# Gate tables built from rounded one-hots, with the gate split into a high and a low part

## What is computed

```
qry  = (x @ w_q)                                  # 8 heads, two halves of 128
s    = qry . sub_keys                             # 128 scores for each half
s_top, i_top = top_k(s, 16)                       # per half
best, pos = top_k(all 256 sums of the two, 16)    # per head
expert = i * 128 + j                              # i from the first half, j from the second
gate = softmax(best)                              # 16 per head, so 128 choices a token
hid  = gelu(x . u_tab[expert])
out  = sum over choices of gate * hid * v_tab[expert]
```

## Time and profile before

| | |
|---|---|
| median of 3 runs | 1135.03 us (1134.43 to 1135.56) |
| span of the profiled execution, first to last instruction | 1132.8 us |
| TensorE busy in the span | 1091.1 us, 96% |
| VectorE, ScalarE, GpSimd busy | 815.5, 555.7 and 589.1 us |
| stage with the gate tables | 417.8 to 750.4 us |
| mean granted TensorE clock | 0.990 of full speed |

### The profile page before, as it was taken

The page is one execution under the profiler, slowest core; times in us unless marked ns, Lnnn a source line. Parts: engine busy times, 40 slices in busy tenths (PEclk is TensorE's granted clock), DMA queues, the critical chain, the costliest instruction groups (busy, mean ns, idle before and its releaser), DMA issues.

```text
span 1132.8 us, 20715 instructions
## 1 busy us (share of the span) xinstructions
PE 1091.1 (96%) x6734; PEld 966.9 (85%) x6734; DVE 815.5 (72%) x1398; ACT 555.7 (49%) x898; POOL 589.1 (52%) x452
## 2 busy tenths in 40 slices
PE   6999999986999999999989999999999999999995
PEld 4887887675999999999989999997888888888884
DVE  4347656365899988888997888976666666666666
ACT  4347544542345555455555555554444444444442
POOL 5484345443322346666556667655555555555554
PEclk9999999997999999999999999999999999999998
DMA  6655344342545554444434444446555555555552
GB/s 200 240 187 167 130 161 137 111 149 77 166 157 182 169 180 154 162 151 165 157 124 164 149 132 146 134 161 216 192 186 185 185 186 187 187 190 193 186 186 93
DMA packets 52474, 186.51 MB, mean 165 GB/s; under 512 B 6209, under 2 KB 6593, under 8 KB 52433
## 3 DMA queue, kind: packets, MB, share of 16 engines
q1 hardware_dynamic: 51584, 182.87, 48.5%
q0 software_dynamic: 848, 3.15, 0.8%
HBM read 184.94 MB, written 1.05 MB: 164 GB/s over the span
## 4 chain that ended last, share of the span: by engine, by line
PE 84%; DVE 8%; DMA 3%; issue 2%; POOL 2%; ACT 1%; DVEq 0%; SPq 0%; POOLq 0%
PE ps L1150 15%; PE ps L1151 15%; PE ps L1152 15%; PE ps L1450 10%; PE ps L1452 10%; PE ps L1451 10%; PE ps L1410 5%; DVE wlo L717 2%; DMA raw<-w_tiles_in 1%; POOL wlo L346 1%; PE ps L1190 1%; DVE hot L1024 1%; ACT whi L482 1%; DVE sel L1029 1%; PE ps L1377 1%
## 5 line engine op out<-in xcount | busy, mean ns | idle before, releaser
L346 POOL TENSOR_TENSOR wlo<-raw,whi 128x256 fp32r<-128x256 f32 x341 | 440.2, 1292 | 497.7 <-ACT whi L482 497.2
L717 DVE TENSOR_TENSOR wlo<-raw,whi 128x768 fp32r<-128x768 f32 x341 | 361.4, 1060 | 254.5 <-ACT whi L482 253.0
L482 ACT ACTIVATE whi<-raw 128x1024 fp32r<-128x1024 f32 x344 | 364.2, 1059 | 331.4 <-DMA raw<-w_tiles_v 180.4
L1150 PE MATMUL ps<-ahi,whi 128*128 128x256 f32 x1152 | 333.5, 290 | 3.0 <-DVE wlo L717 1.6
L1151 PE MATMUL ps<-alo,whi 128*128 128x256 f32 x1152 | 326.4, 283 | 0.0
L1152 PE MATMUL ps<-ahi,wlo 128*128 128x256 f32 x1152 | 326.2, 283 | 0.0
L1150 PEld LDWEIGHTS ps<-ahi,whi 128*128 128x128 f32 x1152 | 221.4, 192 | 3.8 <-DVE wlo L717 2.0
L1151 PEld LDWEIGHTS ps<-alo,whi 128*128 128x128 f32 x1152 | 221.7, 192 | 0.0
L1152 PEld LDWEIGHTS ps<-ahi,wlo 128*128 128x128 f32 x1152 | 221.2, 192 | 0.0
L1450 PE MATMUL ps<-whi,hhi 128*128 128x512 f32 x512 | 202.4, 395 | 1.1 <-POOL wlo L346 1.1
L1451 PE MATMUL ps<-wlo,hhi 128*128 128x512 f32 x512 | 202.2, 395 | 0.0
(11 more groups left out here) (190 smaller groups left out, 998.3 us busy)
## 6 DMA issues: line engine op xcount, KB each, us to landing
raw<-w_tiles_u SPq DMA_DIRECT2D x128, 512.0 KB, 3.3
raw<-w_tiles_v SPq DMA_DIRECT2D x128, 512.0 KB, 3.3
raw<-w_tiles_in SPq DMA_DIRECT2D x64, 512.0 KB, 3.3
raw<-w_tiles_q SPq DMA_DIRECT2D x16, 512.0 KB, 3.4
raw<-w_tiles_out SPq DMA_DIRECT2D x8, 512.0 KB, 3.3
xraw<-xT SPq DMA_DIRECT2D x4, 256.0 KB, 6.3
xt<-x POOLq DMA_DIRECT2D x1, 1024.0 KB, 5.6
out<-xt SPq DMA_DIRECT2D x4, 256.0 KB, 2.0
```

Source lines behind the costliest of these rows:

```text
L346: pool.tensor_tensor(wlo[:, tile.slot, DVE_COLS:], raw[:, tile.slot, DVE_COLS:], whi[:, tile.slot, DVE_COLS:].bitcast(F32), ALU.subtract)\
L482: act.activation(whi[:, tile.slot, :], raw[:, tile.slot, :], ACT.Copy)\
L717: dve.tensor_tensor(wlo[:, tile.slot, 0:DVE_COLS], raw[:, tile.slot, 0:DVE_COLS], whi[:, tile.slot, 0:DVE_COLS].bitcast(F32), ALU.subtract)\
L1150: pe.matmul(out, ah, bh, start=start, stop=False)
```

## The change

The plain fp32 product of a token becomes two fp32r products that are summed in PSUM. The gate moves from the j side to the i side and is split: `gateT` now has the type fp32r (the rounded gate), `gate_lo` is the fp32 gate less the rounded one. The stationary `hot_j` is the bare one-hot of j, the moving operands are `hot_i`, scaled by the rounded gate, and `hot_lo`, scaled by the rest.

- GpSimd scales the i half instead of the j half (`scale_i`, the same shape).
- ScalarE copies the j half in one instruction as before, and then makes `hot_lo` with four instructions of 128 columns, one for each token, each with that token's `gate_lo` column as its per-partition scale. `hot_lo` has one buffer, so these wait until TensorE has finished the chunk before.
- VectorE computes `gate_lo` once for each half of the tokens.
- TensorE issues eight fp32r products of 128 columns for a chunk, where it issued four plain ones.
- `keys` and `iota` move in SBUF behind the PEER buffers, and `rstd`, `shift` and `gate_warm` become columns of one tensor, which makes room for `hot_lo` and `gate_lo`.

```
-        def scale_j(c):
+        def scale_i(c):
             pool.wait_ge(S["hot_ready"], c + 1)
             if c >= HOTS:
                 pool.wait_ge(S["g_done"], c + 1 - HOTS)
-            pool.tensor_tensor(hot_j[:, c % HOTS, :, :], raw_ij[:, c % HOTS, 1, :, :].rearrange("p j n -> p n j"),
-                               gateT[:, c * BLK:(c + 1) * BLK, None].to_broadcast([P, BLK, P]), ALU.mult)\
-                .then_inc(S["hot_j_ready"], 1)
+            pool.tensor_tensor(hot_i[:, c % HOTS, :, :], raw_ij[:, c % HOTS, 0, :, :].rearrange("p i n -> p n i"),
+                               gateT[:, c * BLK:(c + 1) * BLK, None].bitcast(F32).to_broadcast([P, BLK, P]),
+                               ALU.mult).then_inc(S["hot_i_ready"], 1)
...
-        def widen_i(c):
+        def hot_parts(c):
             act.wait_ge(S["hot_ready"], c + 1)
             if c >= HOTS:
                 act.wait_ge(S["g_done"], c + 1 - HOTS)
-            act.activation(hot_i[:, c % HOTS, :, :], raw_ij[:, c % HOTS, 0, :, :].rearrange("p i n -> p n i"), ACT.Copy)\
-                .then_inc(S["hot_i_ready"], 1)
+            act.activation(hot_j[:, c % HOTS, :, :], raw_ij[:, c % HOTS, 1, :, :].rearrange("p j n -> p n j"), ACT.Copy)
+            if c > 0:
+                act.wait_ge(S["g_done"], c)
+            for k in range(BLK):
+                last = act.activation(hot_lo[:, k, :], raw_ij[:, c % HOTS, 0, :, k], ACT.Copy,
+                                      scale=gate_lo[:, c * BLK + k:c * BLK + k + 1])
+            last.then_inc(S["hot_j_ready"], 1)
...
             own.do(dve.tensor_copy(gateT[:, toks], ps[:, SEL_BANKS[t], 2 * P:3 * P]))
+            own.do(dve.tensor_tensor(gate_lo[:, toks], ps[:, SEL_BANKS[t], 2 * P:3 * P], gateT[:, toks].bitcast(F32),
+                                     ALU.subtract))
...
             for k in range(BLK):
-                last = pe.matmul(ps[:, RING[b], k * P:(k + 1) * P], hot_j[:, b, k, :], hot_i[:, b, k, :],
-                                 start=True, stop=True)
+                o = ps[:, RING[b], k * P:(k + 1) * P]
+                pe.matmul(o, hot_j[:, b, k, :], hot_i[:, b, k, :], start=True, stop=False)
+                last = pe.matmul(o, hot_j[:, b, k, :], hot_lo[:, k, :], start=False, stop=True)
             last.then_inc(S["g_done"], 1)
```

More of the change, by code:

```diff
@@ L206, in layer @@
     ident = place("ident", [P, P])
-    keys = place("keys", [P, 2, NK])
-    iota = place("iota", [P, P])
     stats = place("stats", [P, NT, 2, 6])
     mv = place("mv", [P, NT, 2])
-    rstd = place("rstd", [P, NT])
-    shift = place("shift", [P, 1])
-    gate_warm = place("gate_warm", [P, 1])
+    columns = place("columns", [P, 4])
+    rstd, shift, gate_warm = columns[:, 0:NT], columns[:, NT:NT + 1], columns[:, NT + 1:NT + 2]
     work_at = at[0]
@@ L247, in layer @@
     square = place("square", [P, GDV])
-    assert at[0] <= nc.sbuf_usable_end, at[0]
+    low_end = at[0]
+    assert low_end <= nc.sbuf_usable_end, low_end
     at[0] = work_at
@@ L262, in layer @@
     hot_at = at[0]
-    hot_i = place("hot_i", [P, HOTS, BLK, P])
-    hot_j = place("hot_j", [P, HOTS, BLK, P])
+    hot_i = place("hot_i", [P, HOTS, BLK, P], F32R)
+    hot_j = place("hot_j", [P, HOTS, BLK, P], F32R)
     qs = place("qs", [P, 2, SEQ], alias=hot_at)
@@ L267, in layer @@
     selT = place("selT", [P, 2, SEQ], BF16)
-    gateT = place("gateT", [P, SEQ])
+    gateT = place("gateT", [P, SEQ], F32R)
     iota4 = place("iota4", [P, P, BLK], BF16)
@@ L275, in layer @@
     gsum = place("gsum", [P, PH])
+    late_at = at[0]
+    keys = place("keys", [P, 2, NK])
+    iota = place("iota", [P, P])
+    assert late_at >= low_end, (late_at, low_end)
+    at[0] = late_at
+    hot_lo = place("hot_lo", [P, BLK, P], F32R)
+    gate_lo = place("gate_lo", [P, SEQ])
     assert at[0] <= nc.sbuf_usable_end, at[0]
@@ L457, in _ @@
             if c is not None:
-                scale_j(c)
+                scale_i(c)
             split_lo(Tile(T_U + u + AHEAD))
@@ L681, in _ @@
             if c is not None:
-                widen_i(c)
+                hot_parts(c)
             split_hi(Tile(T_U + u + AHEAD))
```

## The result

The changed kernel takes 1139.45 us (median of 6 runs, 1137.07 to 1139.86) beside 1135.18 us for the kernel before in the same rounds: ratio 1.0036, 95% interval 1.0026 to 1.0046, 0.36% slower, or +4.1 us by the ratio (the two medians lie 4.3 us apart). The forecast was 1139 us. Neither of its two terms came out, though: the products cost nothing where it had +1.8 us, and ScalarE's copies cost more than its +2.1 us. Part of what looks like their cost in the profile is a spell of lower TensorE clock.

What follows compares the result with a forecast made beforehand. TensorE was taken as the bound, except from 545 to 592 us, where VectorE is. Products +1.8 and copies +2.1 give +3.9 us on 1135.03, or 1139 us; range 1117 to 1144 us, chance 0.8.

Steps and rivals of the forecast that it cites:

- the term of the products: TensorE's tables: eight narrow fp32r products cost 0.03 us more a chunk, over 59 chunks +1.8 us (-1.9 to +3.9).
- that of the copies: ScalarE's small copies delay VectorE's tiles in the stretch that VectorE fills: +2.1 us (0 to 5.6).
- The bound, and that the tables are paid in full: TensorE, 96% busy, bounds the kernel; each chunk's tables cost it 0.89 us, 57 us for 64 chunks.
- The distance of narrow fp32r products: On TensorE the weight load sets how closely 128-column products start: 0.115 us, between bounds 0.107 and 0.120.
- my two rows: TensorE product distances the estimate lay between: plain fp32 records 0.111 us apart, fp32r products of 256 columns 0.120.
- ScalarE's copies: Four new 128-column instructions on ScalarE, 0.30 us each, 1.2 us a chunk (0.7 to 1.6), fitting its wait for TensorE.
- The two waits that I had counted: VectorE waits for the late `split_hi` at two chunks of its full stretch: 2 x (1.2 - 0.15) = +2.1 us.
- mostly free: `split_hi` 1.2 us later on ScalarE costs little outside VectorE's full stretch, its result being due over 6 us after ScalarE's start.
- Loads free: Rival on TensorE: moving columns alone set 0.067 us a product, tables take 0.53 us a chunk, 1119 us; chance 0.21.
- Plain rate for narrow fp32r: Rival on TensorE: each narrow product costs a plain one's 0.222 us, tables 1.78 us a chunk, 1189 us; chance 0.10.
- Longer delay: Rival: ScalarE's delay, 1.6 us a chunk, reaches further, with more VectorE-GpSimd collisions from 690 us on, 1147 us; chance 0.09.
- GpSimd, `gate_lo`, the moved tensors: Remaining parts: GpSimd's multiplication worth nothing, VectorE's `gate_lo` covered (0.6 us at most), moved tensors change no instruction.

Runs made afterwards that it cites:

- e4: Changed kernel without ScalarE's four small copies, each fp32r product with 64 stationary columns instead of 128 (half of each table missing): 1113.58 us, ratio 0.981 to before.
- e3: Changed kernel without ScalarE's four small copies, each fp32r product moving 64 columns instead of 128 (half of each table missing): ratio 1.0002 to before.
- e11: Changed kernel with one fp32r product a token instead of two and no small copies, low part of the gate left out: 1110.23 us, ratio 0.9779 to before.
- e2: Changed kernel without ScalarE's four small copies; the second fp32r product of a token reads hot_i once more: ratio 1.0001 to before.

## Why the prediction came out right

The total came out to half a microsecond, and that was luck: the term of the products was 1.8 us too high, that of the copies about 1.0 too low, and the clock, some 0.9 us in the profiled execution, had no term.

**The bound, and that the tables are paid in full:** right. e4 takes 0.36 us off each chunk (6.64 to 6.28) and the time falls by 21 us.

**The distance of narrow fp32r products.** The mechanism was right: the load sets it, and two halves of a product are no gain when each loads its own weights. The size was off. I took 0.115 us and +0.03 us a chunk, between the plain rows and the fp32r rows; it is 0.111, and the term of +1.8 us is 0. The surplus of the 256-column fp32r products (0.120) doesn't appear here; where it comes from no run shows. The lower of my two rows was the right neighbour.

**ScalarE's copies.** 0.30 us from start to start and 1.2 us a chunk were right (1.21), and so were the shrunken wait (0.60) and the place of the loss. Its size was not: +2.1 us against about 3.1 of waiting. The two waits that I had counted came as forecast, 1.01 us at 568.03 and 1.00 at 592.86. What failed is the step before them, that the later `split_hi` is "mostly free" outside the stretch. It cost no time there, but it used up VectorE's lead. Where the stretch begins, before and after:

```profile
543.35 0.96 DVE L717 TENSOR_TENSOR wlo<-raw,whi 128x768 fp32r<-128x768 f32 x1 [0.72 <-ACT whi L482]
```

```profile
545.44 0.96 DVE L727 TENSOR_TENSOR wlo<-raw,whi 128x768 fp32r<-128x768 f32 x1 [0.89 <-ACT whi L487]
```

VectorE waits here in both. But before it takes this tile 0.69 us ahead of the tables of chunk 19 (544.04), and in the changed kernel 0.57 us behind them (544.87). The chain of waits of the changed kernel starts from there (start, us):

```profile
543.17 1.29 ACT hot_lo L663 x4
544.46 0.95 ACT whi L487
...
545.44 0.96 DVE wlo L727
```

TensorE then waits for `hot_lo` at all five chunks from 21 to 25, where it waited at four for `hot_j`. I had also taken the ends of `hot_lo` and `hot_i`, 1.9 and 1.7 us, to be equal; that is worth 0.13 us. On top, the profiled execution lost about 0.9 us to the lower clock, for which the forecast had no term.

**Loads free (0.21):** shown wrong by e3 and e4. The Trainium skill's 81 ns for a load and a product at 128 columns (TensorE: Matmul & The Clock Gate, back-to-back issue gap) fits neither type: fp32r takes 0.111 us here and bf16 0.056. The measurements decide. **Plain rate for narrow fp32r:** the distance of a plain product, 0.222 us, doesn't occur. **Longer delay:** not seen from 690 us on; 26 to 63 is unchanged to 0.04 us, and VectorE's busy time there falls from 59.75 to 53.01 us where more collisions with GpSimd were feared. Nor is VectorE's busy share a need: the forecast took from it that no tile from 690 us on could be quicker than 3.57 us, and e4 runs at 3.40 and e11 at 3.31 there. The rival's 1119 us was therefore worked out some 3 us too high; the forecast's own sum doesn't use it.

**GpSimd, `gate_lo`, the moved tensors:** nothing, as e2 shows, which keeps all three.

## What to carry over

When a product moves no more columns than it loads, count loads, not columns: replacing one two-pass product by two one-pass products keeps the count and gains nothing, while a type with a quick load, or fewer products, gains at once. Work that is put on an idle engine is judged by what stands behind it in that engine's queue, and in the one stretch where the engine that waits for it is full. There count the lead with which that engine arrives, and not only its waits inside: delay that costs nothing for twenty chunks still uses the lead up. Errors of opposite sign can hide behind a total that is right to half a microsecond, so check the terms, and look at the granted clock before a loss is put down to waiting.

## What the runs showed of the hardware

- TensorE's granted clock fell to half for about 3.3 us in the middle of the stage in 7 of the 14 profiled executions (granted clock 0.51 from 593.5 to 596.8 us in the changed kernel's). Products of 256 columns then start 0.21 us apart in place of 0.12, and 19 run in place of 31.
- An fp32r product with 64 stationary and 128 moving columns starts 0.060 us after the one before; with 128 stationary columns it is 0.111, whether 128 or 64 columns move.
- A bf16 load of 128 columns has a record of 0.098 us against 0.192 for fp32r, and with weights read at 8-byte steps 0.112 to 0.118; both start products 0.056 us apart.
- A ScalarE copy of 128 columns with a per-partition scale lasts 0.416 us and the next starts after 0.30.
